# Three held parts of expert rows instead of two, their one-hots turned behind the loop, and all joins on VectorE

## What is computed

```python
    gates = jnp.sum(jax.nn.one_hot(expert, N_EXPERTS, dtype=jnp.float32) * w[..., None], axis=1)
    hg = jnp.einsum('td,edf->tef', h, w_gate)
    hu = jnp.einsum('td,edf->tef', h, w_up)
    act = jax.nn.silu(hg) * hu * gates[..., None].astype(h.dtype)
    return jnp.einsum('tef,efd->td', act, w_down)
    # in _layer, and at the end:
    x = x + gate2 * moe_out.reshape(x.shape)
    y_sample = _rmsnorm(xs, final_norm_w)
```

## Time and profile before

| what | value |
|---|---|
| median of 3 runs | 580.58 us (578.71 to 581.12) |
| the profiled execution | 576.9 us, of which the span is 575.1 us |
| TensorE products | 487.0 us busy, 85% of the span |
| TensorE weight loads, beside the products | 238.8 us, 42% |
| VectorE | 226.6 us, 39% |
| ScalarE | 146.7 us, 26% |
| GpSimd | 109.3 us, 19% |
| transfers | 165.13 MB, mean 287 GB/s |

### The profile page before, as it was taken

One profiled execution on the slowest core, in us unless ns is written; L12 is line 12 of the kernel. 1 busy time (PEld: TensorE's weight loads), 2 busy tenths in 40 slices (PEclk: granted clock), 3 DMA queues, 4 the chain that ended last, 5 costly groups with the idle time before them and its releaser, 6 DMA issues. The chain is left out here.

```text
span 575.1 us, 8706 instructions
## 1 busy us (share of the span) xinstructions
PE 487.0 (85%) x3246; PEld 238.8 (42%) x3247; DVE 226.6 (39%) x542; ACT 146.7 (26%) x281; POOL 109.3 (19%) x185
## 2 busy tenths in 40 slices
PE   2779979999787999969799997898797798797873
PEld 1225668564686544656523332232232232232221
DVE  2689977999843105573400010100000000000086
ACT  3546873710367201420300110000000000001043
POOL 3000514888911061023000000000000000000341
PEclk9987999999888999975989999998998899898898
DMA  8990050856699920218999959399999999999732
GB/s 293 377 391 6 15 188 12 303 211 229 215 387 403 410 94 0 111 71 308 425 422 421 425 199 369 123 376 425 426 429 423 419 426 421 424 421 419 233 125 109
DMA packets 38149, 165.13 MB, mean 287 GB/s; under 512 B 2760, under 2 KB 3528, under 8 KB 32352
## 3 DMA queue, kind: packets, MB, share of 16 engines
q1 hardware_dynamic: 31408, 146.32, 64.3%
q10 hardware_dynamic: 4288, 10.33, 4.7%
q0 software_dynamic: 2416, 7.98, 3.7%
HBM read 153.28 MB, written 11.34 MB: 286 GB/s over the span
## 5 line engine op out<-in xcount | busy, mean ns | idle before, releaser
L712 PE MATMUL psum<-arena 128*64 128x512 f32 x672 | 159.6, 630 | 18.8 <-DVE arena L1516 12.8
L712 PEld LDWEIGHTS psum<-arena 128*64 128x64 f32 x672 | 52.3, 145 | 115.1 <-issue 107.1
L725 PE MATMUL psum<-arena 128*64 128x512 f32 x336 | 81.0, 626 | 17.4 <-ACTq L1044 14.4
L1521 DVE TENSOR_TENSOR arena<-arena,psum 128x256 f32<-128x256 f32 x21 | 8.8, 421 | 186.0 <-ACT arena L1017 186.0
L1771 POOL DMA_INDIRECT arena<-sorted_outputs,src_u x6 | 5.7, 955 | 277.7 <-DMA sorted_outputs<-arena 276.2
L725 PEld LDWEIGHTS psum<-arena 128*64 128x64 f32 x336 | 26.4, 144 | 65.0 <-issue 65.0
L1017 ACT ACTIVATE arena<-psum 128x256 f32<-128x256 f32 x21 | 8.1, 384 | 149.7 <-PE psum L712 149.7
L641 PE MATMUL psum<-arena 128*128 128x512 f32 x96 | 41.5, 592 | 0.0
L641 PEld LDWEIGHTS psum<-arena 128*128 128x128 f32 x96 | 18.2, 190 | 22.3 <-issue 22.0
L505 PE MATMUL psum<-arena 128*128 128x388 f32 x64 | 24.8, 537 | 1.1 <-ACT arena L880 1.1
L1033 ACT ACTIVATE arena<-psum 128x512 f32<-128x512 f32 x19 | 11.3, 597 | 49.6 <-PE psum L725 48.3
(11 more groups left out here) (315 smaller groups left out, 642.3 us busy)
## 6 DMA issues: line engine op xcount, KB each, us to landing
arena<-in_w_gate SPq DMA_DIRECT2D x16, 2048.0 KB, 16.2
arena<-in_w_up SPq DMA_DIRECT2D x16, 2048.0 KB, 21.1
arena<-in_w_down SPq DMA_DIRECT2D x16, 2048.0 KB, 18.0
arena<-in_w_mod SPq DMA_DIRECT2D x12, 2048.0 KB, 15.2
arena<-in_w_in SPq DMA_DIRECT2D x3, 2048.0 KB, 19.5
sorted_outputs<-arena ACTq DMA_DIRECT2D x38, 128.0 KB, 7.5
arena<-in_w_out SPq DMA_DIRECT2D x2, 2048.0 KB, 14.5
arena<-modulation_rows ACTq DMA_DIRECT2D x3, 1024.0 KB, 10.6
```

The lines of the kernel that those rows point to most:

```text
L712: last = mm(bank[0][HALF * t:HALF * t + HALF, :], xs[:, k, :], gu[:, :, k, t * 256:t * 256 + 256], start=(k == 0), stop=(k == KD - 1))
L725: last = mm(bank[4][HALF * h:HALF * h + HALF, :], hiddenT[:, s * P + t * HALF:s * P + t * HALF + HALF], dn[:, 2 * t + s, h * 512:h * 512 + ...
```

## The change

The last pass of expert 14 is held too, so that there are three held parts: part 0 is the last pass of expert 14, part 1 the held pass of expert 15, part 2 its last pass. `PREV` is 14. On each engine:

- VectorE makes nine one-hots instead of six, with more small operations for the bounds of the parts; the two comparisons of each run over 64 elements where they ran over 128, and the sum writes both halves. Its loop ends one expert earlier, and the step of expert 14 stands behind it, with the scaling of part 0 (2 x 128x512) ahead of the multiply of expert 15's first pass. All three joins are on VectorE; in the branch for one more pass (64 < n <= 128) they all stand ahead of the multiply of that pass.
- TensorE no longer turns one-hots ahead of the loop; it turns nine behind the loop, ahead of the second pass of expert 15. Five of the six products of part 0 stand between that pass's gate/up and down products, the sixth behind the last down product, followed for each tile by the products of part 1 and part 2.
- ScalarE's loop covers experts 0 to 11, and 12 to 14 are written out. It issues the loads of the gate rows, their halves and the norm's weights behind the gate of expert 14's first pass and ahead of the evacuation of expert 13; SyncE no longer does. The copies of the turned one-hots (three, of 4, 4 and 1 blocks) follow the gate of expert 15's first pass. Expert 14's last pass is copied to `ystage` and not written to DRAM. One row for each tile is weighed, all three ahead of the gate of the second pass.
- GpSimd's gathers wait for the writes of expert 13 and for the gate/up products of expert 14 (their destination lies over that weight set); its own join is gone. `hTs` has 960 columns instead of 1024, and the memset of its end is shorter.
- The semaphores `s_in`, `earlier_done` and `count_done` are merged into `d_in` and `tri_done`.

The core of the diff; the changes of ScalarE's branches are as told above, and so is `join`:

```diff
@@ -159,19 +160,19 @@
-        late_y = view(slot(2), 2, 2, 512)
-        onehots = view(slot(8) + 2048, 2, NT, P)
-        late_T = view(F + 14080, 2, NT, P)
+        late_y = view(slot(2), 3, 2, 512)
+        onehots = view(F + 13568, 3, NT, P)
+        late_T = view(slot(0) + 2048, 3, NT, P)
@@ -401,13 +403,6 @@
-            sp.wait_ge(S("downed"), 14 * PASSES + 1)
-            sp.dma_start(g2rows.rearrange("p a b -> p (a b)"),
-                         modd[5].rearrange("s d -> (s d)").partition_broadcast(P)).then_inc(S("g2_in"), 16)
-            for h in range(2):
-                sp.dma_start(g2halves[HALF * h:HALF * h + HALF],
-                             modd[5][:, h * 512:h * 512 + 512].partition_broadcast(HALF)).then_inc(S("g2_in"), 16)
-            sp.dma_start(fnw, io["final_norm_w"].partition_broadcast(P)).then_inc(S("fnw_in"), 16)
@@ -776,11 +774,6 @@
-            pe.wait_ge(S("onehots_done"), 1)
-            for i in range(2 * NT):
-                last = tr(bank[1 + 2 * (i // 4)][:, (i % 4) * P:(i % 4) * P + P], onehots[:, i // NT, i % NT, :],
-                          ident[:, :])
-            last.then_inc(S("late_ready"), 1)
@@ -798,16 +791,34 @@
-            expert_rest(0, LAST, 5)
...
+            def late_part(part, t, h):
+                half = slice(HALF * h, HALF * h + HALF)
+                return mm(late_bank(t)[:, h, :], late_T[half, part, t, :], late_y[half, part, min(t, 1), :],
+                          start=(part == 0), stop=(part == 2))
...
+            pe.wait_ge(S("onehots_done"), 1)
+            for i in range(3 * NT):
+                last = tr(bank[(1, 3, 7)[i // 4]][:, (i % 4) * P:(i % 4) * P + P],
+                          onehots[:, i // NT, i % NT, :], ident[:, :])
+            last.then_inc(S("late_ready"), 1)
...
+            def first_part():
+                pe.wait_ge(S("late_copied"), 3)
+                for t, h in ((0, 0), (0, 1), (1, 0), (1, 1), (2, 1)):
+                    pe.wait_ge(S("held_scaled"), min(t, 1) + 1)
+                    late_part(0, t, h)
...
+            expert_rest(0, LAST, 5, first_part)
...
-            pe.wait_ge(S("late_copied"), 2)
+            late_part(0, 2, 0)
...
-                for part, ready in ((0, "held_scaled"), (1, "last_scaled")):
-                    pe.wait_ge(S(ready), min(t, 1) + 1)
-                    for h in range(2):
-                        half = slice(HALF * h, HALF * h + HALF)
-                        last = mm(late_bank(t)[:, h, :], late_T[half, part, t, :],
-                                  late_y[half, part, min(t, 1), :], start=(part == 0), stop=(part == 1))
+                pe.wait_ge(S("held_scaled"), min(t, 1) + 3)
+                for h in range(2):
+                    late_part(1, t, h)
+                pe.wait_ge(S("last_scaled"), min(t, 1) + 1)
+                for h in range(2):
+                    last = late_part(2, t, h)
@@ -1072,34 +1077,54 @@
+            with act.Fori(0, 6) as i:
...
-            gate(turn(0, LAST))
...
+            gate(turn(0, PREV))
...
+            act.dma_start(g2rows.rearrange("p a b -> p (a b)"),
+                          modd[5].rearrange("s d -> (s d)").partition_broadcast(P)).then_inc(S("g2_in"), 16)
+            for h in range(2):
+                act.dma_start(g2halves[HALF * h:HALF * h + HALF],
+                              modd[5][:, h * 512:h * 512 + 512].partition_broadcast(HALF)).then_inc(S("g2_in"), 16)
+            act.dma_start(fnw, io["final_norm_w"].partition_broadcast(P)).then_inc(S("fnw_in"), 16)
...
+            expert_rest(PREV, 0)
+            act.wait_ge(S("downed"), turn(PASSES, PREV) + 1)
+            A(ystage[:, 0, :], bank[4][:, :], ACT.Copy).then_inc(S("evacuated"), 1)
...
+            def gate_last():
+                gate(turn(0, LAST))
+                act.wait_ge(S("late_ready"), 1)
+                for i in range(3):
+                    n = (4, 4, 1)[i]
+                    A(late_T.rearrange("p a t c -> p (a t c)")[:, 512 * i:512 * i + n * P],
+                      bank[(1, 3, 7)[i]][:, 0:n * P], ACT.Copy).then_inc(S("late_copied"), 1)
...
+            def weigh(t):
...
-                    act.wait_ge(S("written"), 32 * (turn(0, LAST) + 1))
+                    act.wait_ge(S("written"), 32 * turn(PASSES, PREV))
...
-                A(ystage[:, 0, :], bank[4][:, :], ACT.Copy).then_inc(S("evacuated"), 1)
+                A(ystage[:, 1, :], bank[4][:, :], ACT.Copy).then_inc(S("evacuated"), 1)
...
-                                  ystage[HALF * h:HALF * h + HALF, 0, :]).then_inc(S("late_written"), 16)
+                                  ystage[HALF * h:HALF * h + HALF, 1, :]).then_inc(S("late_written"), 16)
@@ -1561,29 +1582,33 @@
-            pos, start, from_held = g1.rearrange(flat)[:, 0:6], r2[:, 1, LAST:LAST + 1], r2[:, 0, 0:1]
-            held_w, last_w, held_at = (g.rearrange(flat)[:, 0:6] for g in (g2, g3, g4))
-            last_at = sel[:, 2, 0:6]
-            v(stt(from_held, start, -float(HALF), off[:, LAST:LAST + 1], ALU.add, ALU.max))
-            d(ts(held_at, pos, from_held, None, ALU.subtract))
-            v(ts(held_w, pos, from_held, None, ALU.is_ge))
-            d(ts(last_w, pos, start, None, ALU.is_ge))
-            v(stt(mk[:, 0, 0:6], held_w, float(PAIRS), pos, ALU.mult, ALU.max))
+            pos, off_last = g1.rearrange(flat)[:, 0:6], off[:, LAST:LAST + 1]
+            start_prev, start_last, from_held = r2[:, 1, PREV:PREV + 1], r2[:, 1, LAST:LAST + 1], r2[:, 0, 0:1]
+            marks, held = r1.rearrange(flat), sig.rearrange(flat)
+            late = marks[:, 36:42]
+            v(stt(from_held, start_last, -float(HALF), off_last, ALU.add, ALU.max))
+            for i, bound in ((18, start_prev), (24, off_last), (30, from_held), (12, start_last)):
+                d(ts(marks[:, i:i + 6], pos, bound, None, ALU.is_ge))
+            d.settle()
+            d(tt(marks[:, 0:6], marks[:, 18:24], marks[:, 24:30], ALU.subtract))
+            v(tt(marks[:, 6:12], marks[:, 30:36], marks[:, 12:18], ALU.subtract))
+            v(tt(late, marks[:, 0:6], marks[:, 30:36], ALU.add))
+            d(tt(held[:, 0:18].rearrange("p (a b) -> p a b", a=3), marks[:, 0:18].rearrange("p (a b) -> p a b", a=3),
+                 wts[:, 0:6].unsqueeze(1).broadcast_to([P, 3, 6]), ALU.mult))
+            d(stt(mk[:, 0, 0:6], late, float(PAIRS), pos, ALU.mult, ALU.max))
+            for part, bound in enumerate((start_prev, from_held, start_last)):
+                d(ts(held[:, 18 + 6 * part:24 + 6 * part], pos, bound, None, ALU.subtract))
+            v(tt(marks[:, 18:24], late, wts[:, 0:6], ALU.mult))
...
-            d(tt(held_w, held_w, wts[:, 0:6], ALU.mult))
-            v(tt(last_w, last_w, wts[:, 0:6], ALU.mult))
-            d(ts(last_at, pos, start, None, ALU.subtract))
-            d(tt(wts[:, 0:6], wts[:, 0:6], held_w, ALU.subtract))
-            v(tt(held_w, held_w, last_w, ALU.subtract))
-            dve.wait_ge(S("count_done"), 1)
-            counts = count_row.unsqueeze(1).broadcast_to([P, 2, HALF])
-            for part, at, weight in ((0, held_at, held_w), (1, last_at, last_w)):
+            v(tt(wts[:, 0:6], wts[:, 0:6], marks[:, 18:24], ALU.subtract))
+            dve.wait_ge(S("tri_done"), 3)
+            for part in range(3):
...
-                    o = onehots[:, part, t, :].rearrange("p (h j) -> p h j", h=2)
-                    second = tri[:, :].rearrange("p (h j) -> p h j", h=2)
-                    d(ts(o, counts, at[:, t:t + 1], weight[:, t:t + 1], ALU.is_equal, ALU.mult))
-                    v(ts(second, counts, at[:, 3 + t:4 + t], weight[:, 3 + t:4 + t], ALU.is_equal, ALU.mult))
-                    v(tt(o, o, second, ALU.add))
+                    one, two, n = tri[:, 0:HALF], tri[:, HALF:P], 6 * part + t
+                    d(ts(one, count_row, held[:, 18 + n:19 + n], held[:, n:n + 1], ALU.is_equal, ALU.mult))
+                    v(ts(two, count_row, held[:, 21 + n:22 + n], held[:, n + 3:n + 4], ALU.is_equal, ALU.mult))
+                    one, two = (x.unsqueeze(1).broadcast_to([P, 2, HALF]) for x in (one, two))
+                    v(tt(onehots[:, part, t, :].rearrange("p (h j) -> p h j", h=2), one, two, ALU.add))
@@ -1591,12 +1616,21 @@
-            with dve.Fori(0, NE - 1) as e:
+            def to_next(e):
...
+            with dve.Fori(0, PREV) as e:
+                to_next(e)
...
+            to_next(PREV)
+            dve.wait_ge(S("g2_in"), 48)
+            dve.wait_ge(S("evacuated"), turn(PASSES, PREV) + 1)
+            for g in range(2):
+                tt(late_y[:, 0, g, :], ystage[:, 0, :], g2halves[:, g, :], ALU.mult).then_inc(S("held_scaled"), 1)
+            multiply(turn(0, LAST))
@@ -1762,21 +1789,17 @@
-            G.memset(hTs[:, :, PAIRS:SORTED], 0.0).then_inc(S("pad_done"), 1)
...
-            pool.wait_ge(S("written"), 32 * (turn(0, LAST) + 1))
+            G.memset(hTs[:, :, PAIRS:READ], 0.0).then_inc(S("pad_done"), 1)
...
```

(7 more changed lines are left out.)

102 lines of the change are left out of this document (46 added, 56 removed).

## The result

| | before | after |
|---|---|---|
| median of 18 runs each, on one chip | 579.01 us | 585.49 us |
| the profiled execution | 576.9 us | 585.33 us, of which the span is 583.6 us |

The ratio is 1.0124, with a 95% interval from 1.0099 to 1.0149: the change costs 1.2%, 5.7 to 8.6 us. The forecast was 580.4 us with a range up to 583.3, so the result lies beyond the range and on the side of the third rival. Of the ratios in this document, those of e1 to e4 would come out some 0.5% lower over all executions, since 10 of the 23 of the kernel before on their chip lie more than 1.5% above its fastest one and are left out as slow.

The account below looks back on a forecast made before the run. It saw the end bound by VectorE's held-row scalings, then TensorE's late products and the last norm, with TensorE nearly always busy before. Terms: -0.85 + 0 + 1.1 - 0.4 = -0.15 us, giving 580.4 us, range 577.2 to 583.3.

Parts of the forecast that it names:

- the third rival: Last expert: gathers not earlier, expert 13's writes landing at 540; +3.25 us, 583.8 us in all; chance 0.13.
- (a): Code before the expert loop: turn of the hidden rows starts earlier, -0.85 us, bounds -1.5 and +0.35.
- (b): Scaling-row loads moved to ScalarE: issue hidden, expert 15's up weights land in time; 0 us, bound +0.5.
- the cover: ScalarE's four load issues end by 521.8, before the down product its evacuation waits for, 0.6 us to spare.
- the bound of +0.5: Scaling-row loads: under equal queue shares expert 15's up weights land at 531.4, 0.5 us late.
- (c): Last expert: gathers start at 536.6, joins hold the turn until 556.2, last down product later; +1.1 us.
- The 36%: ScalarE's queue share beside SyncE's 64%, taken from an earlier stage; puts expert 13's writes at 536.6.
- the second rival: Equal turns between the queues: weights 0.5 us late, writes land near 532.5; -0.35 us, 580.2 us; chance 0.17.
- the first rival: Filled gap keeps TensorE's clock high in the last expert, turn at 554.4; -2.6 us with (a)'s best bound, 578.0; chance 0.20.
- (d): Late products behind the last down product: shorter wait before the last records, -0.4 us, bounds -1.1 and 0.
- The bound of 540: Last expert: latest gather start considered, if the queue's share is much smaller or its small packets slow.
- The joins decide, at 556.2: Last expert: VectorE's three joins allow TensorE's last turn at 556.2; TensorE alone would be there at 555.5.

Follow-up runs that it names:

- e1: Changed kernel with the four scaling-row loads issued by SyncE between expert 15's gate/up and down weights: 579.46 us, ratio 1.0041 to the kernel before.
- e2: Changed kernel, last expert reordered: VectorE does one join, then the multiply, other joins later; loads stay on ScalarE: 578.11 us, ratio 1.0028 to the kernel before.
- e3: Kernel before, with only the four scaling-row loads moved to ScalarE behind the gate of expert 14's first pass: 583.49 us, ratio 1.0109.
- e4: Kernel before, with only all three joins put on VectorE ahead of the second pass's multiply, GpSimd's join gone: 587.37 us, ratio 1.0161.
- e5: Changed kernel with the five early products of part 0 moved behind the last down product: 588.9 us, ratio 1.0180 to the kernel before.
- e6: Changed kernel with the joins of tiles 1 and 2 left out, so output is incomplete: 580.4 us, ratio 1.0032 to the kernel before.
- e7: Changed kernel, scaling-row loads on SyncE; joins 0 and 1, multiply, then join 2 cut around the last scaling: 576.91 us, ratio 0.9976 to the kernel before.
- e8: Changed kernel with ScalarE's four loads issued directly behind expert 13's writes instead of ahead: 583.7 us, ratio 1.0105 to the kernel before, 4 runs.
- e9: As e7, with join 1 also cut around the multiply and the norm's weights loaded behind the down weights: 576.14 us, ratio 0.9933 to the kernel before.
- e10: The same kernel as e7, timed again on another chip: 577.34 us, ratio 0.9942 to the kernel before.

## Why the prediction was wrong

**(a) Before the loop: mis-sized.** -0.85 us was forecast. From the start of the first expert's gate/up product to the turn of the hidden rows it is 281.21 - 270.32 = 10.89 us against 11.12 before: -0.23. The small operations took 2.36 us (2.4 forecast). A one-hot group took 0.90 and not 0.83, and nine groups make 0.6 us. The 64-wide comparisons take 0.31 each, only 0.03 less than the 128-wide ones of before. The 0.19 that I took was three overlapping operations divided by three; one of them takes 0.25, and it only compares, where these compare and multiply. How much of the 0.06 is the multiplication was not tried.

**(b) The scaling rows: right for the profile, not for the kernel.** ScalarE's issues end at 523.86, ahead of the evacuation at 524.91. They take 2.4 us for the four, the upper end of 0.35 to 0.6 each, and the cover held. The up weights landed in 31.6 us, where 28.3 + 2.8 = 31.1 was forecast, and no wait followed. In e5 and e6 they took 33.2 and 33.4, TensorE waited about 2 us for them, and the bound of +0.5 was passed. In e6 the stretch is 0.5 us shorter than before and the median still 0.3% longer, so such a wait can be part of what the medians lose.

**(c) The last expert: here the prediction failed.** The failed step is "2.36 MB (2304 KB) at 36% of 0.431 MB/us take 15.2 us from 521.4, so they land at 536.6". From the first issue at 521.49 to the gather at 542.71 are 21.2 us, 0.111 MB/us on the average, 26% of 0.431; e2 shows 31% (2.36 MB in 17.6 us). In the times of before the gather is at 542.71 - 2.23 = 540.5: later than the 538 at which the prediction called itself wrong, and where the third rival, "gathers not earlier", had it. That rival had no sum for its 540; it took the landing of expert 14's writes, so its nearness is in part luck.

The 36% was no share. It is an average over a landing of 7.6 us, and for the first part of it ScalarE's queue moved nothing. In 198 to 200 us, when its loads ran beside the last of SyncE's weights, ScalarE's queue moved most of the bytes. Transfer view of these 2 us, kernel before:

```profile
q10 hardware_dynamic: 85, 0.70, 83.7%
q1 hardware_dynamic: 38, 0.13, 16.5%
```

And of 526 to 540 us, kernel after:

```profile
q1 hardware_dynamic: 640, 2.96, 59.8%
q10 hardware_dynamic: 651, 2.09, 41.4%
```

Here ScalarE's queue moved 2.09 MB in 14 us, 0.149 MB/us; the sum had 0.36 x 0.431 = 0.155. That these agree is luck: the share was higher, 41%, and the whole lower, 361 GB/s and not 431. By the sum's own start (521.4, which is 523.6 in the times of after) and rate the gather is 3.9 us late, and by my estimate from these windows the loss lies mostly at the two ends: 1.2 us ahead of 526, when some 0.2 MB were moved and not 0.37; 0.5 us in the 14; and 2.1 us behind 540, where the last 0.09 MB and the release of the gather took 2.7 us and not 0.6.

Every later step of the sum was met: gather to first weighing 6.79 us (6.8), three joins with their start 11.15 (11.1), the turn at 562.29 - 2.23 = 560.1, for which that rival had 559.6.

In the changed kernel the packets went one for one: 234 of SyncE's and 226 of ScalarE's in 520 to 530 us, 640 and 651 in 526 to 540. The bytes did not, because the packets differ in size: 13 KB and 4.8 KB on the average in the first window, 4.6 and 3.2 in the second. The Trainium skill (DMA: Bandwidth & Descriptors, on queues and completion) has each engine drain one packet from a queue before it turns to the next. The trace agrees with that. The equal shares that I made of it in the second rival need packets of equal size, and these were not.

**The clock: not in the sum at all.** The rival had 3.25 us for the loss; measured are 6.0. The difference is made of (a), 0.6; the gather at 540.5 and not 540, 0.5; the handover from turn to down product, 1.50 and not 1.25; and 1.4 us because the last down product takes 5.07 us and not 3.65. The stretches, kernel after (us, busy and count of TensorE, its weight loads, VectorE, ScalarE, GpSimd, then TensorE's granted clock, the share of the transfers and GB/s):

```profile
560.00:565.00 5.00, 1.90 (x6) 0.88 (x8) 3.83 (x6) 0.00 (x0) 0.00 (x0) 0.50 0.02 3
565.00:570.00 5.00, 5.00 (x20) 1.74 (x18) 1.10 (x2) 0.00 (x0) 0.00 (x0) 0.83 0.00 0
```

The granted clock is 0.50 (1.2 GHz) in the 5 us in which the product starts and 0.83 in the next, so it comes back to 2.4 GHz in that stretch. Such a wait on TensorE's path costs itself and this. From the forecast's -0.15 us to the measured 6.0 the terms are the gather 3.9, (a) 0.6, the handover 0.25 and the clock 1.4. I had looked at the clock only as a gain, in the first rival, whose 7.09 us came true and were then spent waiting.

**(d) The late products: right.** From the end of the last down product to the end of the additions are 7.48 us (568.86 to 576.34) against 7.87 (560.03 to 567.90): -0.4, as forecast. The scalings of the held rows take 1.28 us where GpSimd had stretched them to 5.22, and ten late records take 2.85 us (2.6 forecast). Timeline of VectorE, kernel before:

```profile
556.19 5.22 DVE L1660 TENSOR_TENSOR arena<-arena 128x512 f32<-128x512 f32 x2
```

The Trainium skill (SBUF — State Buffer, "two separate sides") holds that a VectorE operation with two SBUF inputs and a GpSimd operation that reads SBUF exclude each other on a shared pair of ports. The trace agrees: 1.28 us for two such products in the changed kernel and in e4, with GpSimd idle, against the 5.22 us of that row, beside GpSimd's L1777.

**Where the weight stood.** I had written that a gather later than 536.75 makes the change a loss, and put the estimate at 536.6. The step that decided was a share taken from one stage, and its rival got 0.13. The bound of 540 stood in the text, and the range stopped short of it. Last, the text never priced the order by itself: it costs some 6 us where the gather comes after 9 us (e4 against before, 43.35 and 37.0), and as much where it comes after 3.5 (e1 against e7, 41.5 and 35.7). "The joins decide, at 556.2" against TensorE's own 555.5 looked like a tie, when one side of it hung on a transfer.

What stays open: what sets the size of the packets and the lower total of 296 to 307 GB/s in 532 to 536 us of the changed kernel; and why the same loads leave the writes 11.8 us in one profile (e2) and 15.5 to 15.9 in four (after, e3, e5, e6). The up weights landed 26.3 us after their issue in e2 and 30.9 to 33.4 us in the four, so the two go together, but what came first is not shown. Open too is whether it is the down weights that hold the gathers for 10.6 us in e1 (argued from the busy queues, not isolated).

## What to carry to other kernels

On an in-order engine, put the short operation that another engine waits for (here 0.4 us of multiply) ahead of long work that hangs on a transfer; cut the long work in steps and place them in the waits that are there anyway. A load that changes its queue delays what is queued behind it there, and whatever waits for that: follow the small writes, not only the large loads. A share of two queues is to be read from a stretch in which both have work, with the packets and the bytes of each. Where a forecast has two paths within 1 us and one of them rests on an estimated transfer, give the case in which it loses most of the weight, and add the price of the low clock to every new long wait on TensorE.

## What the runs showed of the hardware

- The 16-record down product of experts 14 and 15, by TensorE's wait before it or before the turn ahead of it: 3.65 us after waits of up to 2.61 us; 3.65 or 4.99 to 5.35 after 2.69 to 3.09 us (3.65 in e5, e6 and at expert 15 in the kernel before; 5.35 at expert 14 in the kernel before, in after, e2 and e3; 4.99 in e4); and 4.98 to 5.96 after each of six waits from 3.70 to 9.46 us, which is 1.3 to 2.3 us on top of the wait. The Trainium skill (TensorE: Matmul & The Clock Gate, Part 1), by which idleness throttles the array, agrees.
- The two writes of 128 KB of expert 13 land in 5.7 to 7.8 us ahead of loads or on a queue without them (before, e1, e4, e7 to e10), and in 11.8 to 15.9 us behind 2 MB of loads in the same queue (after, e2, e3, e5, e6). Writes of an earlier expert, with no loads ahead in their queue, took 8.8 to 9.3 us in after, e5 and e6.
- While weights on SyncE's queue and the loads on ScalarE's ran side by side, the transfer engines took packets one for one (640 and 651 in 526 to 540 us of after, 487 and 488 in 526 to 538 of e5, 488 and 487 in 527 to 539 of e6), and the bytes followed the size of the packets (2.96 and 2.09 MB in after).
- The same gap of 1.6 us before the second gate/up product was followed by low clock in one profile (8.68 us) and by full clock in e4 (7.09 us after 1.57): a gap of that size can't be priced from one profile.
